# Two layers in one kernel: the transfers that build the weight sums are issued earlier and in another order

## The reference, cut to what matters

```
layer 1: h += (gate_a*(window_attention @ w_a) + gate_b*(latent_attention @ w_b)) @ w_out
layer 2: h += (sigmoid(ga)*(differential_attention @ w_a) + sigmoid(gb)*(window_attention @ w_b)) @ w_out
each   : h += (silu(n @ w_gate) * (n @ w_up)) @ w_down        n = rms_norm(h), w_gate: 1024 x 2816
```

## Time and profile before

| what | value |
|---|---|
| median of 3 runs | 1469.65 us (1466.66 to 1476.88) |
| the profiled execution: time, span | 1473.38 us, 1471.7 us |
| PE busy | 1452.7 us, 99% |
| DVE, ACT, POOL busy | 975.2, 654.3, 258.2 us |
| mean granted clock of PE | 0.997 |
| q1 (SP): moved, share of the 16 DMA engines | 152.24 MB, 36.4% |
| q0 (POOL): moved, share | 83.27 MB, 24.8% |

### The profile page before, as it was taken

One profiled execution on the slowest core, in us unless ns is written; L12 is line 12 of the kernel. 1 busy time (PEld: TensorE's weight loads), 2 busy tenths in 40 slices (PEclk: granted clock), 3 DMA queues, 4 the chain that ended last, 5 costly groups with the idle time before them and its releaser, 6 DMA issues.

```text
span 1471.7 us, 23871 instructions
## 1 busy us (share of the span) xinstructions
PE 1452.7 (99%) x8712; PEld 1253.2 (85%) x8712; DVE 975.2 (66%) x1779; ACT 654.3 (44%) x1175; POOL 258.2 (18%) x260
## 2 busy tenths in 40 slices
PE   9999999999999999999999999999999999999998
PEld 8868786888898898999899777777888988989997
DVE  6678977575776576787744372434767765867875
ACT  5234446535453353465411373544344533534643
POOL 2024536201101100000003675331011001000000
PEclk9999999999999999999999999999999999999999
DMA  7536674249899993663223237653388999736632
GB/s 187 148 100 211 173 133 130 79 111 191 202 328 226 250 217 98 199 184 106 86 86 86 58 101 162 151 188 80 107 186 226 305 218 242 213 95 195 185 104 93
DMA packets 342909, 236.91 MB, mean 161 GB/s; under 512 B 24729, under 2 KB 322837, under 8 KB 342814
## 3 DMA queue, kind: packets, MB, share of 16 engines
q1 hardware_dynamic: 305518, 152.24, 36.4%
q0 software_dynamic: 37216, 83.27, 24.8%
q10 hardware_dynamic: 80, 0.14, 0.0%
HBM read 233.48 MB, written 81.88 MB: 214 GB/s over the span
## 4 chain that ended last, share of the span: by engine, by line
PE 88%; DMA 6%; DVE 3%; ACT 1%; issue 1%; DVEq 0%; SPq 0%; POOL 0%; ACTq 0%
PE psL L2293 37%; PE psL L2520 12%; PE psS L2316 10%; PE psL L2316 6%; PE psS L2293 5%; PE psT L2316 4%; PE psT L2529 2%; DMA stage<-in_w_ffn_up 1%; DMA stage<-in_w_ffn_gate 1%; DMA stage<-in_w_ff_up 1%; PE psL L2655 1%; PE psS L2836 1%; PE psS L2570 1%; PE psL L2791 1%; PE psS L2814 1%
## 5 line engine op out<-in xcount | busy, mean ns | idle before, releaser
L918 ACT ACTIVATE wh<-stage 128x1024 fp32r<-128x1024 f32 (+3 forms) x211 | 203.6, 965 | 362.1 <-PE psL L2293 199.6
L1398 DVE TENSOR_TENSOR wl<-stage,wh 128x1024 fp32r<-128x1024 f32 (+2 forms) x168 | 183.8, 1094 | 57.7 <-ACT wh L918 57.3
L2293 PE MATMUL psL<-hid,wh 128*128 128x512 f32 x672 | 207.3, 390 | 0.0
L2520 PE MATMUL psL<-hn,wh 128*128 128x512 f32 x496 | 165.0, 414 | 0.8 <-DVE yn L2176 0.8
L2293 PE MATMUL psL<-hn,wh 128*128 128x512 f32 x528 | 165.0, 394 | 0.0
L2293 PEld LDWEIGHTS psL<-hid,wh 128*128 128x128 f32 x672 | 125.6, 188 | 26.2 <-DVE wl L1398 0.6
L2293 PE MATMUL psL<-hid,wl 128*128 128x512 f32 x336 | 130.7, 389 | 0.0
L746 POOL TENSOR_TENSOR wl<-stage,wh 128x1024 fp32r<-128x1024 f32 (+1 forms) x43 | 97.7, 2273 | 172.7 <-ACT wh L918 172.7
L2293 PEld LDWEIGHTS psL<-hn,wh 128*128 128x128 f32 x528 | 97.7, 188 | 23.1 <-issue 3.3
L2520 PEld LDWEIGHTS psL<-hn,wh 128*128 128x128 f32 x496 | 84.5, 189 | 24.5 <-issue 11.1
L2293 PE MATMUL psL<-hn,wl 128*128 128x512 f32 x264 | 102.9, 390 | 0.0
(11 more groups left out here) (507 smaller groups left out, 3333.0 us busy)
## 6 DMA issues: line engine op xcount, KB each, us to landing
stage<-in_w_in SPq DMA_DIRECT2D x53, 512.0 KB, 4.0
wsum<-weight_sums_1g SPq DMA_DIRECT2D x18, 512.0 KB, 5.2
wsum<-weight_sums_1u SPq DMA_DIRECT2D x18, 512.0 KB, 5.3
wsum<-weight_sums_2g SPq DMA_DIRECT2D x18, 512.0 KB, 4.7
wsum<-weight_sums_2u SPq DMA_DIRECT2D x18, 512.0 KB, 4.5
stage<-in_w_out SPq DMA_DIRECT2D x16, 512.0 KB, 4.7
stage<-in_w_ffn_down SPq DMA_DIRECT2D x32, 256.0 KB, 3.0
stage<-in_w_ff_down SPq DMA_DIRECT2D x32, 256.0 KB, 3.0
```

The source lines that it names most:

```text
L918: act.activation(wh[:, b, 0:n], stage[:, b, 0:n], ACT.Copy).then_inc(hi[b], 1)
L1398: v.tensor_tensor(wl[:, b, 0:n], stage[:, b, 0:n], wh[:, b, 0:n].bitcast(F32), ALU.subtract).then_inc(lo[b], 1)
L2293: ins = pe.matmul(dst, w[:, b, k * P:(k + 1) * P], x[:, part, k, c0:c1], start=done_ + n == 0, stop=done_ == kc - 1 and n == 2)
L2520: ins = pe.matmul(psL[:, b, :], w[:, b, k * P:(k + 1) * P], hn[:, part_, k, META:], start=k + n == 0, stop=k == KD - 1 and n == 2)
```

## The change

Per layer the same 48 transfers are issued, with the same sources, destinations and sizes. What changes is their order within a layer and their places in POOL's list.

- The order is now a table, `SUM_ORDER`. In layer 1 it is all 16 of part a, n = 0 to 11 of part b, n = 0 to 7 of part c, the last four of b and the last eight of c. In layer 2 it is all of part a, the eight copies of b, the eight copies of c, and then the accumulations of b and of c.
- Layer 1: seven copies stand right behind the load of `biasA`, one by one; the eighth behind `cm8`, two accumulations between the two `low` pairs of `uq1`; the rest of part a and twelve transfers of part b in `gates1`; the eight copies of part c, without waits, among the `mask_bias` steps; twelve accumulations, one by one, after `mix_ok`.
- Layer 2: the eight copies of part a come when PE nears the end of `gu1b` (`mm[0]` at the number of `dn1b`), its eight accumulations when PE nears the end of `gu1c`, six copies of part b behind `dist`; two of b and six of c, without waits, stand among the map steps; then in `gates2` two copies of c, the eight accumulations of b and three of c; five accumulations are left after `mix_ok`.
- SP's wait before the paired loads of a part is for the last transfer of that part in the new order.

```
-SUMS_AT = {1: (0, 2, 4, 6, 8, 10, 12, 14, 16), 2: (8, 10, 12, 14, 16, 19, 22, 24, 26)}
+SUMS_AT = {1: (10, 12, 14, 16, 19, 22, 24, 26, 28), 2: (30, 32, 34, 36, 38, 40, 41, 42, 43)}
+def steps(part, first, last):
+    return [(part, n) for n in range(first, last)]
+SUM_ORDER = {1: [*steps(0, 0, 16), *steps(1, 0, 12), *steps(2, 0, 8), *steps(1, 12, 16), *steps(2, 8, 16)],
+             2: [*steps(0, 0, 16), *steps(1, 0, 8), *steps(2, 0, 8), *steps(1, 8, 16), *steps(2, 8, 16)]}
+def sums_ready(l, part):
+    return len(SUM_ORDER[1]) * (l - 1) + SUM_ORDER[l].index((part, SUM_DMAS - 1)) + 1
...
-                    sp.wait_ge(sums_in, 16 * SUM_DMAS * (3 * l - 3 + part + 1))
+                    sp.wait_ge(sums_in, 16 * sums_ready(l, part))
...
-            def sum_dmas(l, part, first, last):
+            def sum_dmas(l, first, last, one_by_one=False):
...
+                for place in range(first, last):
+                    part, n = SUM_ORDER[l][place]
+                    before = len(SUM_ORDER[l]) * (l - 1) + place
...
-                    if before + n and (n in (0, 8, 12, 14) or 16 * part + n >= 24):
-                        pool.wait_ge(sums_in, 16 * (before + n))
+                    if before and (one_by_one or n in (8, 12, 14) or place in (0, SUM_DMAS)):
+                        pool.wait_ge(sums_in, 16 * before)
...
             windows(fA_dram, LEN_A, biasA, NEAR, 0, NH, biasA_in)
+            sum_dmas(1, 0, 7, one_by_one=True)
             pool.wait_ge(key_taken, 2)
             pool.tensor_copy(cm8[:], ...)
+            sum_dmas(1, 7, 8)
             low_pair("uq1", 0)
+            sum_dmas(1, 8, SUMS_AT[1][0])
             low_pair("uq1", 1)
...
-                if j % 4 == 3:
-                    sum_dmas(1, 1, j // 4, j // 4 + 1)
-            feed_sums(1)
+                if j % 4 == 0:
+                    sum_dmas(1, SUMS_AT[1][-1] + j // 4, SUMS_AT[1][-1] + j // 4 + 1)
+            feed_sums(1, SUMS_AT[1][-1] + 8)
+            pool.wait_ge(mm[0], PAIR0["dn1b"])
+            sum_dmas(2, 0, 8, one_by_one=True)
+            pool.wait_ge(mm[0], PAIR0["dn1c"])
+            sum_dmas(2, 8, 16, one_by_one=True)
...
             pool.iota(dist[:], ...)
+            sum_dmas(2, 16, 22, one_by_one=True)
```

More of the change, by code:

```diff
@@ L750, in low_pair @@
                 low(name, i, 1)
-            def sum_dmas(l, part, first, last):
[L754 to L759, removed]
-                    if before + n and (n in (0, 8, 12, 14) or 16 * part + n >= 24):
-                        pool.wait_ge(sums_in, 16 * (before + n))
+            def sum_dmas(l, first, last, one_by_one=False):
+                for place in range(first, last):
+                    part, n = SUM_ORDER[l][place]
+                    before = len(SUM_ORDER[l]) * (l - 1) + place
+                    t0, t1 = summed_pairs(part)
+                    cols = slice(t0 * P, t1 * P)
+                    second = slice((FPAIRS + t0) * P, (FPAIRS + t1) * P)
+                    upper, lower = slice(0, D // 2), slice(D // 2, D)
+                    if before and (one_by_one or n in (8, 12, 14) or place in (0, SUM_DMAS)):
+                        pool.wait_ge(sums_in, 16 * before)
                     m = "gu"[n % 2]
@@ L805, in _ @@
                     low_pair("gates1", i)
-                sum_dmas(1, 0, SUMS_AT[1][i], SUMS_AT[1][i + 1])
+                sum_dmas(1, SUMS_AT[1][i], SUMS_AT[1][i + 1])
             def mask_bias(j):
@@ L814, in mask_bias, with feed_sums @@
                 pool.tensor_tensor(biasM[:, j % 4, 0:K], biasB[:, h, NKEY - K:NKEY], selm[:, i, 0:K], ALU.subtract).then_inc(biasM_ok, 1)
-            def feed_sums(l):
+            def feed_sums(l, first):
                 pool.wait_ge(mix_ok, KD * l)
-                sum_dmas(l, 1, 8 if l == 1 else 10, SUM_DMAS)
-                sum_dmas(l, 2, 0, SUM_DMAS)
+                sum_dmas(l, first, len(SUM_ORDER[l]), one_by_one=True)
             la_units = list(latent_units())
@@ L895, in _ @@
                 if u % 2 == 0:
-                    sum_dmas(2, 0, u // 2 - 1, u // 2)
-            sum_dmas(2, 0, 7, 8)
+                    sum_dmas(2, 21 + u // 2, 22 + u // 2)
+            sum_dmas(2, 29, SUMS_AT[2][0])
             for i in range(PAIRS["gates2"]):
                 low_pair("gates2", i)
-                part = SUMS_AT[2][i] // SUM_DMAS
-                sum_dmas(2, part, SUMS_AT[2][i] - part * SUM_DMAS, SUMS_AT[2][i + 1] - part * SUM_DMAS)
-            feed_sums(2)
+                sum_dmas(2, SUMS_AT[2][i], SUMS_AT[2][i + 1])
+            feed_sums(2, SUMS_AT[2][-1])
         @block.scalar
```

## The result

The changed kernel takes 1476.03 us in the median of 22 runs (1471.3 to 1480.59), the kernel before 1471.46 in 22 runs (1466.66 to 1476.88). The ratio is 1.0028, with a 95% interval of 1.0017 to 1.0039: slower by some 4.1 us (4.6 by the two medians), where 4.8 less was worked out, and outside the range. The profiled execution of the changed kernel took 1479.51 us with a span of 1477.8, 6.1 more than that of before.

A forecast was written before the change was run, and what follows sets the result against it. PE, busy 99% of the span, bounds the kernel; only its late matmul starts can give time. Terms -6.47 + 3.9 - 2.19 = -4.8 take the profiled 1473.38 to 1468.6; the median, 3.7 lower, gives 1465, range 1457 to 1475.

The forecast's parts named there:

- Two accumulations between the `low` pairs of `uq1`: Just ahead of `gates1`: they hold POOL for two issues of 1.05, between 0 and 2.1 us, taken as 0.
- Part a of layer 1, +3.9: Its pairs share 29 us with accumulations instead of copies and lose 3.9 us, between 0 and 7.1.
- The second theory: Set before the experiments: accumulations beside part a cost more than was worked out and explain the result alone.
- Part b of layer 1, -6.47: No accumulations run beside its pairs any more, so the 6.47 us lost there come back.
- Part a of layer 2, -2.19: Five accumulations end by 1120, before its pairs at 1156.64; gain 2.19 us, between 0 and -2.19.
- The early copies: Seven copies between `biasA` and the `low` of `uq1`: six intervals and the first take 31 of 39 us, cost 0.
- The middle transfers: Fourteen before `vm8`: eight accumulations at 6.75 us, six copies at 4.8; fits with 9 us to spare, cost 0.
- the rival with POOL late: Before the differential attention: `vm8` and `low` of `qa2` late behind fourteen transfers, from about 8.2 us each; 1475 to 1493, chance 0.08.
- The latent attention: Eight larger copies stand where eight stood; POOL only issues them and nobody waits there for their landing; cost 0.
- loads late in `gates1`: Rival: each of the 8 pairs of tiles in `gates1` comes 1.48 us late, 11.8 in all; 1477, chance 0.05.
- The loss only moves: Rival: part a loses 7.1 us and the copies in front of part c 2.19; 1470, no change, chance 0.15.
- The rule on turns between queues: DMA engines alternate queues by packet; if turns alone decided, the +3.9 beside part a would be 0 and the sum 1461.

The follow-up runs named there:

- second experiment: The changed kernel with the two accumulations between the `low` pairs of `uq1` moved behind the first pair of `low` steps of `gates1`: 1470.43 us, ratio 0.9988 to before.
- first experiment: The kernel before plus layer 1's eight early copies and two accumulations between the `low` pairs of `uq1`, all else as before: 1478.18 us against 1471.96, ratio 1.0046.
- the fourth: The changed kernel, two `uq1` accumulations moved into `gates1` and part c's last four in layer 1 held until near part a's down product: 1466.57 us, ratio 0.9956.
- eighth experiment: The kernel before with the change of layer 2 alone, layer 1 keeping its order and places: 1468.93 us, ratio 0.9974 to before.
- ninth experiment: The changed kernel with two 512 KB copies of part a in place of the two accumulations between the `low` pairs of `uq1`: 1470.41 us, ratio 0.9988 to before.
- third experiment: The changed kernel with the last four 1024 KB accumulations of layer 1 held until PE nears part a's down product: 1473.53 us, ratio 1.0003 to before.
- the seventh: The changed kernel with the last two accumulations of part c of layer 1 held until PE nears part a's down product: 1474.98 us, ratio 1.002 to before.

## Why the prediction was wrong, by its own steps

**The step that failed** is "Two accumulations between the `low` pairs of `uq1` hold POOL for 2 issues of 1.05: between 0 and 2.1, and I take 0". It priced the issuing engine alone. That price was right: PE waits 0.35 for POOL's `wl` there, and 0.26 before. What was left out is the other queue. The transfers share the 16 engines with SP's loads, and the next load was a small one with no tile of cover, in front of other work in ACT's list. Measured: +6.58 and +6.78, gone when the two transfers move (second experiment), present when only the early part is made (first). The upper end of 2.1 was too low as well. Added to the sum of -4.8 this one term gives +1.8. PE pausing in `gates1` was named as a sign of being wrong; the pause came, just ahead of the first product.

**Part a of layer 1, +3.9 between 0 and 7.1.** The mechanism was right, pauses behind late loads of the pairs, on `part_x` as named and as often on `wsl`. The size is not a constant: with the last three accumulations of part c beside them the pairs lost 5.55, 2.32, 4.08, 5.49, 2.77 and 5.99 in six executions, 4.4 in the mean. Nor is it one rate: 24 us were shared with accumulations in the second of these and 31 to 33 in the others, which makes 0.085 to 0.19 per us. The two rates behind the middle value (0.176 and 0.089) were each from one execution of a quantity that varies so; the first profile after happens to lie at the upper rate. That +3.9 lies near the mean is partly luck. The second theory is refuted as the whole cause, since the second experiment keeps this loss and is no slower than before, but it is a part: the fourth differs from the second by it.

**Part b of layer 1, -6.47,** measured -6.48 and -6.20; but with before's order of these transfers it lost only 3.81 in the first and 3.27 in the eighth experiment's execution. The one row lay at the upper end. **Part a of layer 2, -2.19,** measured -2.03 and -2.91; before's order lost 1.29 in the first experiment. The 2.19 is 0.16 too high: it took the end from the chain (1199.14), where PE's own first matmul of the down product starts at 1198.98. **Part b of layer 2** was not in the sum. The last two accumulations of before's order run into it, and it lost 0 and 1.85 in the two executions of before and 2.21 in the first experiment; with the new order it lost nothing.

**The zeros.** The early copies fitted: the six intervals took 30.8 us in all, as worked out (31), and the copies were done before `uq1`. The middle transfers fitted, with 7.16 where 6.75 was extended, and the limit of 8.2 was not reached; the rival with POOL late did not occur. The latent attention cost 0.4, not 0: each copy now stands behind the first of four mask steps in place of the fourth, and the runs with before's places (before twice, the first and the eighth experiment) take 58.9 there, those with the new ones 59.3 to 59.4. Which step is late there was not tried. The copies beside part c cost nothing in most executions, 1.41 once and 0.36 once.

**What it adds up to.** With the means over these executions the terms are +6.7 (end of `uq1` to end of `gates1`), +0.4 (latent attention), +4.4, -4.9, -2.1 and -1.4 (the pairs), together +3.1 without the clock at the start. The ratio gives +4.1, with 2.5 to 5.7 as its interval. So these terms are enough; whether the late clock is in the medians too, they cannot tell.

**The rivals.** The time came out as for loads late in `gates1` (1477), but that rival meant eight pairs of tiles each 1.48 late, and inside `gates1` nothing of the kind is seen: all is one load ahead of its first product. "The loss only moves" (1470) is what remains once that load is mended (1470.43). The rule on turns between queues that the prediction weighed can be held against this load. The Trainium skill ("DMA: Bandwidth & Descriptors", Queues, rings and completion order) has a DMA engine change between queues at each packet. With turns alike in length the load would land in about twice its quiet time, an estimate of 4.2 from 2.1. Behind 512 KB copies it stayed under that (2.9), behind 768 KB copies and one accumulation it came near it (4.3 and 4.1), behind two accumulations it was far over (6.9 to 7.5), so equal turns do not price an accumulation. Why an accumulation lasts longer and holds the load, no run here shows.

**What stays open:** why the clock rose late at the start of both profiles of the changed kernel (2.3 and 3.0 us); whether the loss of the pairs is a rate or begins once a lead is used up; why it varies between executions.

## What to carry to other kernels

When a transfer is moved, ask which loads of the other queue are issued while it is in flight, how small they are, and what stands behind their consumer in its engine's list; the issuing engine's hold is the smaller part. Accumulating transfers belong beside phases whose loads have a whole tile of cover; in the tight place here two 512 KB copies made no pause, two 768 KB copies one of 1.49. A loss read from one execution is one sample: profile the kernel twice before a term of 2 to 6 us is written to two decimals.

## What the runs showed of the hardware

- The landing of one 128 KB load with other work on POOL's queue: 2.1 us with nothing there, 2.9 behind two 512 KB copies, 4.1 behind one 512 KB accumulation, 4.3 behind two 768 KB copies, 6.9 to 7.5 behind two 512 KB accumulations.
- Pauses of PE of 4.0 to 4.7 us came with a granted clock of 0.66 to 0.83 in 100 to 110 us and cost 1.6 to 2.7 us more; pauses of 1.26 and 1.49 at the same place, seven of 0.26 to 0.85 within 46 us, and one of 2.16 in the ninth experiment's pairs left the clock at 1.00.
- Three accumulations of 1024 KB beside the four entries of part a cost 2.3 to 6.0 in six executions. Beside the down product behind them, whose tiles have more cover, accumulations of that size cost nothing in four executions (before twice, the first and the third experiment) and 0.92, 1.02 and 1.2 in three (the fourth, the eighth and the seventh).
